# Gate and up products taken chunk by chunk instead of in runs of wide and narrow products

## What is computed

```python
def swiglu(x, w_gate, w_up, w_down):
    return (jax.nn.silu(x @ w_gate) * (x @ w_up)) @ w_down

for l in range(DEPTH):                       # first block, DEPTH = 2
    h = h + 0.5 * swiglu(rms_norm(h, ffn1_norm[l]), ffn1_w_gate[l], ffn1_w_up[l], ffn1_w_down[l])
    h = h + hybrid_mixer(rms_norm(h, mix_norm[l]), ...)
    h = h + 0.5 * swiglu(rms_norm(h, ffn2_norm[l]), ffn2_w_gate[l], ffn2_w_up[l], ffn2_w_down[l])
...                                          # second block, in each of its 2 layers
    gu = h @ w_ffn_gu
    ffn = (jax.nn.silu(gu[..., :D_FF_2]) * gu[..., D_FF_2:]) @ w_ffn_down
```

## Time and profile before

| | us |
|---|---|
| median of 3 runs | 1905.99 |
| span of the profiled execution | 1904.5 |
| TensorE busy with matmuls (PE) | 1892.4 (99%) |
| granted TensorE clock, mean over the span | 0.999 of 2.4 GHz |
| TensorE loading weights (PEld, beside the matmuls) | 1637.8 (86%) |
| VectorE busy | 1340.0 (70%) |
| ScalarE busy | 967.8 (51%) |
| GpSimd busy | 161.4 (8%) |

### The profile page before, as it was taken

One profiled execution on the slowest core, in us unless ns is written; L12 is line 12 of the kernel. 1 busy time (PEld: TensorE's weight loads), 2 busy tenths in 40 slices (PEclk: granted clock), 3 DMA queues, 4 the chain that ended last, 5 costly groups with the idle time before them and its releaser, 6 DMA issues.

```text
span 1904.5 us, 26155 instructions
## 1 busy us (share of the span) xinstructions
PE 1892.4 (99%) x10937; PEld 1637.8 (86%) x10940; DVE 1340.0 (70%) x1485; ACT 967.8 (51%) x1216; POOL 161.4 (8%) x158
## 2 busy tenths in 40 slices
PE   9999999999999999999999999999999999999998
PEld 7888879988888888898888888888888888888887
DVE  7877687877687767868776555568765655568763
ACT  5444656544444446665434665455444665455442
POOL 0000522100000006121000200000000110000000
PEclk9999999999999999999999999999999999999999
DMA  7555542454555554334554443445545443445452
GB/s 284 208 185 177 187 150 106 163 190 178 189 198 179 188 182 177 133 112 177 194 187 165 164 171 133 167 165 188 194 168 185 137 176 133 161 171 188 177 185 102
DMA packets 47491, 327.28 MB, mean 172 GB/s; under 512 B 5520, under 2 KB 5520, under 8 KB 11536
## 3 DMA queue, kind: packets, MB, share of 16 engines
q1 hardware_dynamic: 46512, 323.25, 47.1%
q10 hardware_dynamic: 864, 2.38, 0.3%
HBM read 324.56 MB, written 1.05 MB: 171 GB/s over the span
## 4 chain that ended last, share of the span: by engine, by line
PE 98%; DVE 1%; ACT 1%; issue 0%; DMA 0%; POOL 0%; DVEq 0%; POOLq 0%; ACTq 0%
PE ps L536 34%; PE ps L540 18%; PE ps L524 10%; PE ps L526 10%; PE ps L525 10%; PE ps L530 2%; PE ps L832 2%; PE ps L787 1%; PE ps L789 1%; PE ps L788 1%; PE ps L798 1%; PE ps L531 1%; PE ps L821 1%; PE ps L553 1%; PE ps L708 1%
## 5 line engine op out<-in xcount | busy, mean ns | idle before, releaser
L330 ACT CAST w_hi<-raw 128x2048 fp32r<-128x2048 f32 (+4 forms) x314 | 580.7, 1850 | 585.9 <-PE ps L540 352.2
L337 DVE TENSOR_TENSOR w_lo<-raw,w_hi 128x2048 fp32r<-128x2048 f32 (+4 forms) x314 | 700.3, 2232 | 245.0 <-ACT w_hi L330 242.2
L536 PE MATMUL ps<-x_hl,w_hi 128*128 128x512 f32 x1968 | 494.2, 393 | 0.0
L536 PEld LDWEIGHTS ps<-x_hl,w_hi 128*128 128x128 f32 x1968 | 353.7, 189 | 63.6
L540 PEld LDWEIGHTS ps<-x_hl,w_lo 128*128 128x128 f32 x1968 | 268.5, 190 | 19.3
L540 PE MATMUL ps<-x_hl,w_lo 128*128 128x256 f32 x1968 | 274.3, 282 | 0.0
L524 PE MATMUL ps<-w_hi,x_hl 128*128 128x512 f32 (+3 forms) x672 | 262.5, 391 | 0.0
L526 PE MATMUL ps<-w_hi,x_hl 128*128 128x512 f32 (+3 forms) x672 | 254.3, 378 | 0.0
L525 PE MATMUL ps<-w_lo,x_hl 128*128 128x512 f32 (+3 forms) x672 | 253.6, 377 | 0.0
L1783 DVE TENSOR_REDUCE ffn_tmp<-ps 128x512 f32<-128x1024 f32 x132 | 161.3, 1223 | 102.6 <-PE ps L540 101.9
L536 PE MATMUL ps<-hid_hl,w_hi 128*128 128x512 f32 x836 | 212.9, 394 | 0.0
(11 more groups left out here) (288 smaller groups left out, 2204.9 us busy)
## 6 DMA issues: line engine op xcount, KB each, us to landing
raw<-in_parts SPq DMA_DIRECT2D x278, 1024.0 KB, 4.8
raw<-in_parts SPq DMA_DIRECT2D x20, 768.0 KB, 4.1
raw<-in_parts SPq DMA_DIRECT2D x4, 928.0 KB, 4.6
raw<-in_parts SPq DMA_DIRECT2D x4, 864.0 KB, 4.4
raw<-in_parts SPq DMA_DIRECT2D x6, 512.0 KB, 3.6
raw<-in_parts SPq DMA_DIRECT2D x4, 576.0 KB, 3.8
const<-in_const ACTq DMA_DIRECT2D x1, 1093.0 KB, 5.1
h<-in_x_t SPq DMA_DIRECT2D x1, 1024.0 KB, 7.8
```

The source lines that it names most:

```text
L330: nc.scalar.copy(w_hi[:, i % RING, 0:n_of(i)], raw[:, i % RING, 0:n_of(i)]).then_inc(high_ready, 1)
L337: nc.vector.tensor_tensor(w_lo[:, s, 0:n], raw[:, s, 0:n], w_hi[:, s, 0:n].bitcast(F32), ALU.subtract).then_inc(low_ready, 1)
L536: nc.tensor.matmul(ps[:, bank, :], w_h(c), hl(c).rearrange("p x n -> p (x n)"), start=start and c == 0, stop=False, skip_group_check=True)
```

## The change

All gate and up parts that are not taken by the chunkwise loop use the pair order. For each chunk c and each half f come the wide and the narrow product, and the banks alternate. The part waits for its low half (`part_ready`, that is `low_ready`) at its start, and no more for `high_ready`. The statistics products and the transposes, which stood between the two halves of a part, stand ahead of chunk 4, which is again after 16 of the part's 32 products. The down parts keep the run order.

```diff
                 for p in range(2 * CHUNKWISE[s], 2 * STEPS):
                     i = i0 + p
-                    by_half = p > 0 and i > 1
-                    if by_half:
-                        pe.wait_ge(high_ready, i + 1)
-                    elif i > 1:
+                    if i > 1:
                         part_ready(i)
                     if p >= 3:
                         pe.wait_ge(up_free, u0 + p - 2)
                     hi, lo = view(w_hi, i), view(w_lo, i)
-                    order = [(c, f) for f in range(2) for c in range(KC)]
-                    if p == 0 or i == 1:
-                        order = [(c, f) for c in range(KC) for f in range(2)]
-                    else:
-                        order = []
-                        for f in range(2):
-                            if p == stats_at and f == 1:
+                    for c, f in [(c, f) for c in range(KC) for f in range(2)]:
+                        if c == KC // 2 and f == 0:
+                            if p == stats_at:
                                 pe.wait_ge(const_in, 16)
                                 stats_sum(STATS_FFN)
-                            if p == stats_at + 1 and f == 1:
+                            if p == stats_at + 1:
                                 pe.wait_ge(root_ready, due("root_ready"))
                                 to_rows(STATS_FFN, rstd)
-                            if s == LAST and f == 1 and p in (6, 9, 12, 15):
+                            if s == LAST and p in (6, 9, 12, 15):
                                 turn_h(p // 3 - 2)
-                            m = matmul_run(pair_banks(p) + f, KC, lambda c: hi[:, c, f * P:(f + 1) * P], lambda c: lo[:, c, f * P:(f + 1) * P],
-                                           lambda c: x_hl[:, c, :, :], True, True, i + 1 if by_half and f == 0 else None)
-                    for c, f in order:
                         if i == 0 and c % 2 == 0 and f == 0:
                             pe.wait_ge(*((first_lo, c // 2 + 1) if c < 6 else (low_ready, 1)))
```

## The result

The changed kernel takes 1911.54 us (median of 6 runs, 1908.91 to 1912.79) against 1906.18 us of the kernel before beside it; the ratio is 1.0026, with a 95% interval of 1.0016 to 1.0035. It is slower by some 5 us, in the direction of the forecast and less than its 1915.1. What no number of the forecast had is the spread of one kernel's runs: six runs of the kernel before lie within 0.6 us, six of the changed one within 3.9.

The account below looks back on a forecast made before the run. TensorE, busy for 99% of the span, was taken to bound the kernel. On 1904.5 us, slow pair pace +7.8 and two waits for low halves +1.3 gave +9.1, to 1915.1 us; range 1902.5 to 1917.

Parts of the forecast that it names:

- stops: TensorE waiting for late low halves near 348 and 865 us: two of 0.65 us, +1.3 us, bounds 0 and 1.5.
- moved statistics products: Middle of a part: still after 16 of 32 matmuls, same time to 0.03 us, so cost 0.
- the banks: Both banks of a part done at its end; VectorE's reduction waited for that already, so cost 0.
- the ring: Ring slot of a part, released by the last matmul in either order, so cost 0.
- the released wait: Wait for the high half, one of three in a part, goes away; taken as 0.
- The two paces: Pair stretches in the trace: slow 353.2 and fast 347.0 ns a pair, run order 349.2 between; held until TensorE stops.
- I take the slow pace.: 123 moved gate and up parts at 353.2 ns a pair, 0.063 us more each, +7.8 us.
- rival (b): Both paces, stage by stage: 350.7 ns a pair, 1910.1 us, anything from 1905 to 1913; chance 0.24.
- (a): Fast pace in all moved parts, 347.0 ns a pair: -4.4 + 1.3 = -3.1 us, to 1902.9; chance 0.23.
- (c): Product order costs nothing, pace stays 349.2 ns a pair, only +1.3 us remains, to 1907.3; chance 0.05.
- (d): Alternating banks drop TensorE's clock to 1.2 GHz: upper bound +690 us; chance under one in a hundred.
- The likeliest case: Slow pace nearly everywhere in the moved parts, 351.9 to 354 ns a pair: 1912.5 to 1917 us; chance 0.45.

Follow-up runs that it names:

- kernel with the settled entry: Changed kernel with one part of each stage, after the two with statistics products, in run order; 1915.54 us, ratio 1.0046.
- run-order kernel: Kernel before, its run order kept, but each part waits for its low half at its start; 1907.75 us, ratio 1.0007.
- snake order: Kernel before, parts without statistics products or transposes: 16 wide then 16 narrow products, odd parts narrow first, low half awaited at start; 1903.66 us, ratio 0.9983.
- 16 and 16: Kernel before, but parts without statistics products or transposes take 16 wide products, then 16 narrow ones; 1904.19 us, ratio 0.9991.
- two and two: Changed kernel with both wide products of a chunk ahead of its two narrow ones; 1906.31 us, ratio 1.0001.

## Why the prediction was right or wrong

**The bound, and the terms.** Right: TensorE alone bounds the kernel, and the sum of pace and stops is the whole difference. The moved statistics products, the banks, the ring and the released wait cost nothing that the stage table shows.

**The two paces.** Right in size: 353.2 and 347.0 ns a pair were read from 131 pairs, and 353.3 and 346.7 were found in some 2000; also that a rhythm holds once it is taken, and that the run order lies between. It ends not only where TensorE stops, as the forecast has it, but also at a few other products between the pairs.

**"I take the slow pace."** This is the step that failed. The slow rhythm was there in four stages of six in the first profile and in three, one of them in part, in the second, not nearly everywhere; the time that the step gives, 1915.1, is that of the kernel with the settled entry (1915.5), where all stages are slow. The reasoning counted how many pairs of the trace were slow, and let the stretches that enter from settled narrow products stand for all. That entry is slow indeed, but in the changed kernel it sets only the first part; a stop (in two stages) and the statistics products (in all) cut the stretch, and the forecast itself said that the trace has no pairs behind those. What these cuts do to each rhythm is in the table above: 18 of its 42 stages went on fast. With that unknown, the mixture, rival (b), was the better first choice: its 1910.1, with 1905 to 1913 as its range, holds all 16 runs (1907.8 to 1912.8). I gave it 0.24. That the time came out in the direction of the forecast and at more than half of its size is in part luck of the executions: the first set is 5.4 us slower where 9.1 was forecast, the second set of the same file 2.5.

**The stops.** Right: two, of 0.49 us lateness each, at the two places named. 2 x 0.65 = 1.3 was expected; in the changed kernel the first cost 0.54 + 0.1, and the run-order kernel shows 1.2 in its span and 1.5 in its medians.

**The other rivals.** (a) The fast pace everywhere did not come by itself, but it can be had in five stages, and then, with the stops taken away and the snake order in the sixth, wins by 3.5 us. (c) An order that costs nothing is refuted by the five orders measured: 5.547 and 5.653 (pairs), 5.557 (snake), 5.567 (16 and 16), 5.573 (two and two), 5.587 (run order) us for the same 32 products. The rule of the Trainium skill, "TensorE: Matmul & The Clock Gate", section "Back-to-back issue gap", that an isolated product of N columns takes N/2.4 + 2.5 ns gives an estimated 216 and 109 ns; settled products here took 226.7 and 120.0, each some 11 ns more, and the rule has no turns in it. (d) The clock stayed at 1.00 in all windows shown, whatever the order of the banks.

**The chances.** The range, 1902.5 to 1917, held both the medians and each run. Slower by over 0.2% had 0.60, and the median of the first set is slower by 0.28%; in the second set it is 0.13%, with the same code. Where a kernel has several rhythms, a chance for one number hides that its executions differ by more than the bound of 0.2%: the 16 runs spread over 5 us. The likeliest case's own range was also too narrow at its lower end: a pace of 351.9 ns with no stops gives 1911.3, and 1912.5 needs both stops.

**What is open.** Why a turn from narrow to wide costs 20 ns, and what in TensorE keeps a three-pair cycle going, no view shows. The rhythm of the first pairs of a stage differs between executions of one file, and with it, by the table, all that follows up to the transposes of the last stage. What it depends on is not known. The third stage came in at 230 and 117 in all seven profiles and was fast behind line 580 in all of them; in the other five the entry varied, in the second and the fourth right behind their stops. Whether the two added products, put at the third step of the slow cycle (233), would leave it slow was not tried. The transposes left it slow 19 times of 20 behind 241, and fast once; why that once is open.

## What to carry to other kernels

Where TensorE is the bound, read the pace from the distances between starts in each steady stretch, for each order in which the same products already occur, and look whether two stretches of one order agree: if they don't, the spread belongs in the forecast, and the mixture is its centre. Group products of one kind: each turn from wide to narrow products and back cost 20 ns in long runs, and the order with the fewest turns (snake) gave its gain in each of its 11 runs, while the finest alternation could be best or worst. A wait moved ahead of its use cost only where the copy was late, here in 2 of 123 parts, and those can be found beforehand by laying the copies' ends against the parts' starts.

## What the runs showed of the hardware that was not expected

- One and the same alternation of a 512-column and a 256-column product, each with its own 128x128 weights, ran in two steady rhythms, 346.7 and 353.3 ns a pair, at the full clock, for over 100 us each.
- Which one it is was set by what preceded it, and reproducibly: from settled narrow products slow in all six stages of the kernel with the settled entry; after two added small products fast in all five stages, twice; after one exchange of two products fast in six stages of six behind the step of 236, and slow 93 times of 93 behind that of 241; behind the two cuts by statistics products one outcome for each of five states, in 42 stages of seven profiles.
- Settled runs cost 226.7 ns for 512 columns and 120.0 ns for 256 columns; a turn there and back adds 20 ns, of which the wide products bear 28 and the narrow ones give back 8.
- A stop of TensorE costs about 0.1 us more than the time for which it waits, which shows as the distance from the first product to its successor, 0.33 to 0.34 us instead of 0.23 to 0.24.
